# Convolved feed-forwards: the low part of ten weight units per layer is made by a transfer inside SBUF

## The reference, cut to what matters

```
h = rms_norm(x, norm_ffn_g[l])
u = causal_depthwise_conv(h @ ffn_w_up[l], ffn_conv_w[l], ffn_conv_b[l])     # 1024 -> 5632, width 3
x = x + (silu(u[..., :2816]) * u[..., 2816:]) @ ffn_w_down[l]                # 2816 -> 1024
```

## Time and profile before

| | |
|---|---|
| time, median of 2 runs | 1215.81 us (1215.68 to 1215.93) |
| span of the profiled execution | 1214.1 us |
| what lies around the span, median less span | 1.7 us |
| TensorE busy | 1205.5 us (99%) |
| VectorE busy | 903.9 us (74%) |
| ScalarE busy | 671.1 us (55%) |
| POOL busy | 51.3 us (4%) |
| DMA: bytes moved | 220.40 MB, mean 182 GB/s |
| granted TensorE clock, mean | 0.999 |

### The profile page before, as it was taken

How to read it: one execution, slowest core, us unless ns; L and a number is a source line. 1 busy time by engine, 2 the same in 40 slices (tenths; PEclk the granted TensorE clock), 3 DMA queues, 4 the chain that set the end, 5 groups by cost and what they waited for, 6 DMA issues and landing times.

```text
span 1214.1 us, 17930 instructions
## 1 busy us (share of the span) xinstructions
PE 1205.5 (99%) x7099; PEld 1048.0 (86%) x7099; DVE 903.9 (74%) x1105; ACT 671.1 (55%) x807; POOL 51.3 (4%) x101
## 2 busy tenths in 40 slices
PE   9999999999999999999999999999999999999998
PEld 7888888888899888888888889999888888999986
DVE  5566465568886685566988986988887998698886
ACT  7655354445466664444648556555655755566553
POOL 2000000000010000000010020000001011000000
PEclk9999999999999999999999999999999999999999
DMA  9644645545654335554555454455574435555550
GB/s 349 232 164 168 223 147 200 194 163 196 243 191 166 131 141 206 207 179 168 193 214 174 139 177 161 152 205 174 174 262 161 140 107 184 191 179 180 196 196 35
DMA packets 32568, 220.40 MB, mean 182 GB/s; under 512 B 3888, under 2 KB 4048, under 8 KB 6768
## 3 DMA queue, kind: packets, MB, share of 16 engines
q1 hardware_dynamic: 29888, 212.33, 49.3%
q0 software_dynamic: 1664, 5.41, 1.3%
q10 hardware_dynamic: 944, 1.64, 0.4%
HBM read 218.31 MB, written 1.05 MB: 181 GB/s over the span
## 4 chain that ended last, share of the span: by engine, by line
PE 92%; DVE 6%; DMA 1%; issue 0%; POOL 0%; ACT 0%; ACTq 0%; POOLq 0%; DVEq 0%
PE acc L1850 20%; PE acc L1852 20%; PE acc L1851 20%; PE tb L1878 3%; PE tb L2521 3%; PE tb L2520 3%; PE acc L2520 3%; PE acc L2521 3%; PE tb L2518 3%; PE acc L2518 3%; DVE cacc L1534 3%; DVE wlo L1143 1%; PE acc L2158 1%; PE acc L2160 1%; PE acc L2161 1%; PE tb L1850 1%
## 5 line engine op out<-in xcount | busy, mean ns | idle before, releaser
L1143 DVE TENSOR_TENSOR wlo<-raw,whi 128x2048 fp32r<-128x2048 f32 x184 | 417.3, 2287 | 131.8 <-ACT whi L592 131.8
L592 ACT ACTIVATE whi<-raw 128x2048 fp32r<-128x2048 f32 (+1 forms) x198 | 368.4, 1882 | 56.5 <-PE acc L1852 43.9
L1850 PE MATMUL acc<-whi,xth 128*128 128x512 f32 x704 | 279.8, 397 | 0.6 <-DVE xtl L1241 0.5
L1852 PE MATMUL acc<-whi,xtl 128*128 128x512 f32 x704 | 274.7, 390 | 0.0
L1851 PE MATMUL acc<-wlo,xth 128*128 128x512 f32 x704 | 274.3, 390 | 0.0
L1850 PE MATMUL acc<-whi,yth 128*128 128x512 f32 (+1 forms) x428 | 169.0, 395 | 0.0
L1852 PE MATMUL acc<-whi,ytl 128*128 128x512 f32 (+1 forms) x428 | 166.6, 389 | 0.0
L1851 PE MATMUL acc<-wlo,yth 128*128 128x512 f32 (+1 forms) x428 | 166.4, 389 | 0.0
L1850 PEld LDWEIGHTS acc<-whi,xth 128*128 128x128 f32 x704 | 132.3, 188 | 28.0 <-DVE wlo L1232 1.3
L1852 PEld LDWEIGHTS acc<-whi,xtl 128*128 128x128 f32 x704 | 132.2, 188 | 28.1
L1851 PEld LDWEIGHTS acc<-wlo,xth 128*128 128x128 f32 x704 | 132.4, 188 | 25.7
(11 more groups left out here) (407 smaller groups left out, 1919.3 us busy)
## 6 DMA issues: line engine op xcount, KB each, us to landing
raw<-in_stream SPq DMA_DIRECT2D x200, 1024.0 KB, 5.0
rb<-in_rel_rows POOLq DMA_DIRECT2D x8, 256.0 KB, 2.9
x<-in_x_in ACTq DMA_DIRECT2D x4, 256.0 KB, 7.4
raw<-in_stream SPq DMA_DIRECT2D x2, 512.0 KB, 9.3
gs_sb<-in_gs_row POOLq DMA_DIRECT2D x1, 1024.0 KB, 7.6
frow<-in_fin_row POOLq DMA_DIRECT2D x2, 512.0 KB, 6.0
raw<-in_stream SPq DMA_DIRECT2D x2, 256.0 KB, 7.0
ws_sb<-in_ws_t POOLq DMA_DIRECT2D x1, 512.0 KB, 7.7
```

Source lines behind the costliest of these rows:

```text
L592: act.activation(whi[:, s, c0:UNIT], raw[:, s, c0:UNIT], ACT.Copy).then_inc(hi_ready, 1)
L1143: dve.tensor_tensor(wlo[:, s, :], raw[:, s, :], whi[:, s, :], ALU.subtract).then_inc(lo_ready, 1)
L1850: pe.matmul(o, xh, wh, start=first, stop=False)
L1852: return pe.matmul(o, xl, wh, start=False, stop=last)
```

## The change

Ten units per layer are named in a list, `SENT`: the units 9, 11, 13, 15, 17, 19 and 21 of the up-projection (the second halves of the steps 4 to 10) and 23, 25 and 27 of the down-projection, counted from U1. None of them is one of the seven-product units. For these
- ScalarE makes, right after `whi = round(raw)`, a second copy `wlo = round(-raw)`, which is the negated high part, and counts `hi_ready` only after it;
- POOL waits for that count and starts a DMA from `raw[slot]` to `wlo[slot]` that adds onto what is there: `wlo = -whi + raw`. It counts one of two semaphores, `lo_sent`, by turns; each DMA waits for the last but one before it;
- VectorE's `lo(U)` returns without doing anything;
- whoever waited for `lo_ready` of such a unit (SP before it loads into the slot again, TensorE) waits for its `lo_sent`; the counts of `lo_ready` leave these units out.

SP's loop of loads is written out in place of a loop on the engine. Three pairs of semaphores in the mixers are merged into one each, to make room for the new ones.

```diff
+SENT = tuple(U_MIX + PER_LAYER * l + 15 + u for l in range(2)
+             for u in (9, 11, 13, 15, 17, 19, 21, 23, 25, 27))
...
+        def wait_lo(eng, U, t=0):
+            if U in SENT:
+                i = SENT.index(U)
+                eng.wait_ge(lo_sent[i % 2], 16 * (i // 2 + 1))
+            else:
+                eng.wait_ge(lo_ready, U + 1 - sum(V <= U for V in SENT) + 4 * t)
...
-            groups = TOTAL // SLOTS - 1
-            with sp.Fori(0, groups) as t:
-                for j in range(SLOTS):
-
-                    sp.wait_ge(lo_ready, SLOTS * t + j + 1)
-                    sp.dma_start(raw[:, j, :], stream[SLOTS * t + (SLOTS + j)]).then_inc(raw_ready[j], 16)
-            for u in range(SLOTS * (groups + 1), TOTAL):
-                sp.wait_ge(lo_ready, u - SLOTS + 1)
+            for u in range(SLOTS, TOTAL):
+                wait_lo(sp, u - SLOTS)
                 sp.dma_start(raw[:, u % SLOTS, :], stream[u]).then_inc(raw_ready[u % SLOTS], 16)
...
+            def send_lo(U):
+
+                i, s = SENT.index(U), U % SLOTS
+                pool.wait_ge(hi_ready, U + 1)
+                if i >= 2:
+                    pool.wait_ge(lo_sent[i % 2], 16 * (i // 2))
+                pool.dma_start(wlo[:, s, :].bitcast(F32), raw[:, s, :], accum_op=ALU.add).then_inc(lo_sent[i % 2], 16)
...
                     pool.tensor_scalar(kdiag[:, m, :], ident[:, :], rms(STATS[5 + 2 * l], m), None, ALU.mult).then_inc(r_dg, 1)
+                for U in SENT:
+                    if gu(l) <= U < gu(l + 1):
+                        send_lo(U)
...
-                act.activation(whi[:, s, c0:UNIT], raw[:, s, c0:UNIT], ACT.Copy).then_inc(hi_ready, 1)
+                made_hi = act.activation(whi[:, s, c0:UNIT], raw[:, s, c0:UNIT], ACT.Copy)
+                if U in SENT:
+                    made_hi = act.activation(wlo[:, s, :], raw[:, s, :], ACT.Copy, scale=-1.0)
+                made_hi.then_inc(hi_ready, 1)
...
             def lo(U, t=0):
 
-                if U >= TOTAL:
+                if U >= TOTAL or U in SENT:
                     return
...
                     for half in range(2):
                         s = (U1 + 2 * j + half) % SLOTS
-                        pe.wait_ge(lo_ready, U1 + 2 * j + half + 1)
+                        wait_lo(pe, U1 + 2 * j + half)
```

More of the change, by code:

```diff
@@ L249, in two_blocks_kernel @@
         hi_ready, lo_ready, unit_used = sem("hi_ready"), sem("lo_ready"), sem("unit_used")
+        lo_sent = [sem(f"lo_sent{i}") for i in range(2)]
         m0_done, out_group = sem("m0_done"), sem("out_group")
@@ L274, in two_blocks_kernel @@
         rb_ld, rb_ok = sem("relbias_loaded"), sem("relbias_masked")
-        t_sq, t_d2, t_ms, t_v, t_r, t_y, t_tr, t_g, t_hi, t_lo = (
-            sem("moba_" + n) for n in ("o_squared", "den_squared", "o_summed", "o_meaned", "o_rms", "o_normed",
+        t_sq, t_d2, t_v, t_r, t_y, t_tr, t_g, t_hi, t_lo = (
+            sem("moba_" + n) for n in ("o_squared", "den_squared_and_o_summed", "o_meaned", "o_rms", "o_normed",
                                        "o_transposed", "gained", "hi", "lo"))
@@ L284, in two_blocks_kernel @@
         x_ltr, x_bn, x_ag, x_lms, x_lr, x_nrm, x_btr, x_sl = (
-            sem("conv_ln_" + n) for n in ("transposed", "stats", "mean", "var", "rstd", "normed", "back", "silu"))
+            sem("conv_ln_" + n) for n in ("transposed", "stats_then_head_sums", "mean", "var", "rstd", "normed", "back", "silu"))
         x_ev = sem("mix_kept")
@@ L289, in two_blocks_kernel @@
                                       "log", "log_a", "cumsum"))
-        x_qktr, x_G, x_tab, x_e1, x_gd, x_e2, x_qg, x_kd, x_kb = (
-            sem("gla_" + n) for n in ("qk_transposed", "G_kept", "factors", "exp_G", "G_diff", "exp_diff", "q_decayed",
-                                      "k_decayed", "far_scaled"))
+        x_qktr, x_G, x_tab, x_e1, x_gd, x_e2, x_qg, x_kb = (
+            sem("gla_" + n) for n in ("qk_transposed", "G_kept", "factors", "exp_G", "G_diff", "exp_diff", "qk_decayed",
+                                      "far_scaled"))
         x_at0, x_A, x_Am, x_X, x_Xc, x_o, x_oc = (
             sem("gla_" + n) for n in ("masked_zeroed", "scores", "scores_masked", "cross", "cross_kept", "o", "o_kept"))
-        x_osq, x_oss, x_oms, x_or, x_ytr, x_yg, x_yh, x_yl = (
-            sem("head_" + n) for n in ("squared", "summed", "meaned", "rms", "y_transposed", "y_gained",
+        x_osq, x_oms, x_or, x_ytr, x_yg, x_yh, x_yl = (
+            sem("head_" + n) for n in ("squared", "meaned", "rms", "y_transposed", "y_gained",
                                        "y_hi", "y_lo"))
@@ L591, in hi @@
                 c0 = 512 if is_seven(U) else 0
-                act.activation(whi[:, s, c0:UNIT], raw[:, s, c0:UNIT], ACT.Copy).then_inc(hi_ready, 1)
+                made_hi = act.activation(whi[:, s, c0:UNIT], raw[:, s, c0:UNIT], ACT.Copy)
+                if U in SENT:
+                    made_hi = act.activation(wlo[:, s, :], raw[:, s, :], ACT.Copy, scale=-1.0)
+                made_hi.then_inc(hi_ready, 1)
             def sums_hi(e, i):
                 f, h, _ = w_sums(e, i)
-                act.wait_ge(lo_ready, down_at(e) + sevens(e)[i] + 1)
+                wait_lo(act, down_at(e) + sevens(e)[i])
                 act.activation(h[:, :], f[:, :], ACT.Copy).then_inc(side_hi, 1)
@@ L1568, in _ @@
                 dve.wait_ge(x_e2, l + 1)
-                dve.tensor_tensor(df, tb[3][:, :], df, ALU.mult).then_inc(x_kd, 1)
+                dve.tensor_tensor(df, tb[3][:, :], df, ALU.mult).then_inc(x_qg, 1)
                 dve.wait_ge(x_tab, l + 1)
-                dve.wait_ge(x_qg, 2 * l + 2)
-                dve.wait_ge(x_kd, l + 1)
+                dve.wait_ge(x_qg, 3 * l + 3)
                 k5, q5 = (z[:, :, :].rearrange("p a (m c t) -> p (a m) c t", c=4, t=GCH) for z in (dG, eG))
@@ L1616, in _ @@
                     dve.bn_stats(bnst[:, m, 0:6], tb[3][:, m * 256:(m + 1) * 256]).then_inc(x_bn, 1)
-                    dve.wait_ge(x_bn, 2 * l + m + 1)
+                    dve.wait_ge(x_bn, 3 * l + m + 1)
                     dve.bn_aggr(mvv[:, m, :], bnst[:, m, 0:6]).then_inc(x_ag, 1)
@@ L1626, in _ @@
                 dve.tensor_reduce(stat[:, 96:104], osq[:, :, :].rearrange("p m (h d) -> p (m h) d", d=DV), AX.X,
-                                  ALU.add).then_inc(x_oss, 1)
-                dve.wait_ge(x_oss, l + 1)
+                                  ALU.add).then_inc(x_bn, 1)
+                dve.wait_ge(x_bn, 3 * l + 3)
                 dve.tensor_scalar(stat[:, 80:88], stat[:, 96:104], 1.0 / DV, EPS, ALU.mult, ALU.add).then_inc(x_oms, 1)
@@ L1677, in _ @@
                 dve.tensor_reduce(stat[:, 256:264], msq[:, :].rearrange("p (c d) -> p c d", d=DH), AX.X,
-                                  ALU.add).then_inc(t_ms, 1)
-                dve.wait_ge(t_d2, l + 1)
-                dve.wait_ge(t_ms, l + 1)
+                                  ALU.add).then_inc(t_d2, 1)
+                dve.wait_ge(t_d2, 2 * l + 2)
                 dve.scalar_tensor_tensor(stat[:, 104:112], stat[:, 256:264], 1.0 / DH, stat[:, 248:256], ALU.mult,
@@ L1860, in in_group @@
                     if m == 0:
-                        pe.wait_ge(lo_ready, U + half + 1 + 4 * t)
+                        wait_lo(pe, U + half, t)
                     if norm is not None:
@@ L1898, in seven @@
                 w = [slice(512 * b, 512 * b + 512) for b in range(4)]
-                pe.wait_ge(lo_ready, U + j + 1)
+                wait_lo(pe, U + j)
                 ready(j)
@@ L2021, in first_step @@
                     if m == 0 and kt % 4 == 3:
-                        pe.wait_ge(lo_ready, kt // 4 + 1)
+                        wait_lo(pe, kt // 4)
                     elif m == 0:
@@ L2150, in kq_step @@
                     s = (U_KVQ + 2 * j + half) % SLOTS
-                    pe.wait_ge(lo_ready, U_KVQ + 2 * j + half + 1)
+                    wait_lo(pe, U_KVQ + 2 * j + half)
                     for f in range(4):
@@ L2269, in k_step @@
                 def k_step(hooks={}):
-                    pe.wait_ge(lo_ready, U0 + 3)
+                    wait_lo(pe, U0 + 2)
                     pe.wait_ge(x_gl, l + 1)
```

## The result

The changed kernel takes 1251.6 us (median of 2 runs, 1251.3 to 1252.0) against 1215.8: 1.029 times, 95% interval 1.028 to 1.031. I had forecast 1223.0 and a range up to 1241, so the time lies outside it, on the slower side.

A forecast was written before the change was run, and what follows sets the result against it. TensorE, busy 1205.5 of 1214.1 us, was taken as the bound. Late first sends (3.4) plus unit 11 (0.2) gave 3.6 us per layer, 7.2 in all: span 1221.3, plus 1.7 to the median, 1223.0 us; range 1214.5 to 1241.

The forecast's parts named there:

- nothing can be won here: Whole kernel: only 8.6 us are not TensorE's, none in the changed stages; faster by something unseen had chance 0.01.
- ScalarE's copies are covered: Feed-forward stages: 20 negated copies, 36 us in all, cost nothing beyond each send starting 1.8 us later.
- the transfer's work: Each adding DMA: reads two operands per word written, so 2 x 2.5 = 5.0 us of the DMA engines.
- The first send: Unit 9 of each layer: reserve 5.4 us against 8.8 to landing, so 3.4 us late.
- X: Each send: time from the negated copy's end to the count on `lo_sent`, taken as 8.8 us, bounds 4.8 and 12.
- The fixed part: Each send: landing time apart from moving data, 2.9 less 0.6, 2.3 us; with 5.0 of transfer, 7.3 alone.
- for unit 11 I took 0.2 us: Second send of each layer: landing 12.3 at worst against reserve 10.8, 1.5 late or nothing; 0.2 us taken.
- That stall moves TensorE alone: After the late first send: every later reserve grows by 3.4 us.
- from unit 17 on ... the reserve stays at ... 11.8 us: Later up-projection sends: time from negated copy to first matmul needing the unit stays at 11.8 us.
- The transfer engines run out: Rival, steps with sends: DMA engines bound above 6.5 us per send; at 10 us, 1279 us; chance 0.16 including slot chain.
- The same rival's other sentence: Same rival, later sends: X above 11.8 us alone makes each send late; at X = 15, 1260 us; shared chance 0.16.
- POOL held up by VectorE: Rival, sends: descriptor building waits for VectorE's two-operand SBUF reads, adding 2.3 to 3.3 us to X; 1229 us, chance 0.06.

The follow-up runs named there:

- alone in its place, at unit 17: Changed kernel with only unit 17 of each layer sent: 1216.1 us, 1.0001 times the kernel before.
- unit 9 alone: Changed kernel with only unit 9 of each layer sent: 1228.9 us, 1.0110 times the kernel before.
- the smaller lists: Changed kernel with fewer units sent: from unit 17 on, six per layer, 1227.5 us; units 17, 21 and 25 only, three per layer, 1216.5 us.
- list from 17 on: Changed kernel with the sent units beginning at unit 17, six sends per layer: 1227.5 us, 1.0103 times the kernel before.
- plain copies: Changed kernel with sends that copy without the addition: 1223.5 us with all sends, 1215.7 us with sends from unit 17 on.

## Why the prediction was wrong

**Right:** that nothing can be won here (no kernel came out faster), that ScalarE's copies are covered, that the mixers' merged waits and the unrolled loop cost nothing, and the transfer's work (5.25 us for my 5.0). The first send, too: X was 9.7 us for my 8.8, the wait 4.5 us for my 3.4. The fixed part and the transfer were nearly right: alone in its place, at unit 17, a send took 7.1 to 8.5 us for my 7.3. One term was right by luck: for unit 11 I took 0.2 us, and it cost nothing in one layer and 0.3 in the other, but its send took 14 us, more than my worst case of 12.3, and only the low clock behind the first wait had given it that time.

**Wrong, first: a term left out.** "That stall moves TensorE alone" ended the sum for a late send. Behind a wait of 4.5 us the granted clock was 0.52 for about 5 us, and cost another 2.4 us; behind the waits of 4.6 and 4.2 us with unit 9 alone it cost 1.6 and 2.2 us. The sum took no such price from anywhere; the rows of before have no wait of that length between full stretches. With it and the measured X the first sends come to 6.65 us per layer for my 3.4.

**Wrong, second: the later sends.** The step "from unit 17 on ... the reserve stays at ... 11.8 us", with X = 8.8 against it, put them all out of danger. Of its two sides the reserve was about right (from issue to first use, 11.3 us for my 11.8 at unit 21, 10.0 for my 10.8 or more at unit 27); X was not. Issued beside a pair of loads a send took 12.9 to 14.3 us. I had worked out such a number myself for unit 11 ("12.3 at worst"), from two loads beside a send, and then took nearly nothing for it and did not carry it to the units behind, where a pair of loads and a send met again at the units 13, 21 and 27. In place of the 0.2 us that the sum had for all of them, the sends behind the first cost 18.2 - 6.65 = 11.6 us in the first layer.

**Why the rival was priced wrongly.** "The transfer engines run out" named the place, but set the point at which it begins at 6.5 us of work per send, where the mean load of a step reaches 11.52 us. At 5.25 the mean is only 2 x 2.5 + 5.25 = 10.3 us, and TensorE already lost 12 us with the six later sends per layer. The mean is not the limit. The windows show the work in bunches: DMA shares of 0.53 (785 to 790), 0.58 (885 to 890) and 0.39 (900 to 905) stand right beside others of 0.9 to 1.06. My reading, which no run isolates, is that each transfer must be over before the next link of the slot's loop (send, load, `hi`, negated copy) can start. The same rival's other sentence, that the loss shows at X above 11.8, held in the main: the median send was under it, and behind the first of each layer TensorE waited for the units 13, 21 and 27, all above it; of those below it, one cost a wait of 0.6 us.

**POOL held up by VectorE** did not show: the issues took 0.85 to 0.98 us, all alike (the one at 842.10, with VectorE's product of two SBUF operands inside it from 842.36 on, 0.85), and a lone send landed as the sum without such a term has it. The Trainium skill ("SBUF — State Buffer", "Who interferes with whom") says that a VectorE instruction with two SBUF inputs contends with what GpSimd reads from SBUF, not with what it only writes, and infers that building descriptors needs the write side; these issues agree with it.

How much of the later loss is the crowded send itself and how much the late load behind it stays open; the runs show only that both go when either the density or the work per send is halved.

## What to carry to other kernels

A transfer is hidden if it lands before its user at that place, with what else is in the queues at that moment. So work out the reserve of the first use, before the feeding engines have gained on the bound one, and the landing time in a crowd, not the median. Where the bound engine never waits, relief of another engine is worth nothing, and a wait that is added can cost twice: the wait and the clock behind it. And a mean load of the DMA engines of 90% (10.3 of 11.52 us) is not 10% of room: look at what is issued in the same microsecond.

## What the runs showed of the hardware

- A DMA with addition from SBUF to SBUF took twice the engines' work of a plain one of the same size (5.25 and 2.5 us of all 16 for 1 MB), and its issue on POOL 0.86 us in place of 0.53. The twelve and the six sends of the smaller lists give 5.4 and 5.3 us each.
- After TensorE had stood still for 4.5 us, its clock was granted at the lower level for some 5 us of full work; after a wait of 2.05 us too: from 818.8 to 822.0 the matmuls start 0.21 us apart, beginning 1.6 us after work had begun again. A wait of 1.94 us had a fall behind it as well (changed kernel, at 1211.15). After the waits of 1.53 us the windows show 1.00, and after one of 2.78 us as well (list from 17 on, at 846.34). So the length of the wait alone does not tell.
- A send of 1 MB with addition took 12.9 to 14.3 us in the changed kernel when issued beside two loads of 1 MB, and 8.1 to 10.2 otherwise. Half the size saved the first send 1.3 us of 9.7. The smallest landing of a run was 4.5 or 5.1 us for plain copies, and 6.9 to 9.4 for full ones with addition.
